# Attention's row maxima: four columns turned by one product into four padding rows, placed by a masked multiply on VectorE

## What is computed

```python
def causal_block_attention(q, k, v, log_decay_cum=None):
    T = q.shape[1]
    scale = q.shape[-1] ** -0.5
    ...
    for blk in range(T // Q_BLOCK):
        lo, hi = blk * Q_BLOCK, (blk + 1) * Q_BLOCK
        s = jnp.einsum('bqhd,bkhd->bhqk', q[:, lo:hi], k[:, :hi]) * scale
        if log_decay_cum is not None:
            s = s + (cum[:, :, lo:hi, None] - cum[:, :, None, :hi])
        mask = (lo + jnp.arange(Q_BLOCK))[:, None] >= jnp.arange(hi)[None, :]
        p = jax.nn.softmax(jnp.where(mask, s, -jnp.inf), axis=-1)
        outs.append(jnp.einsum('bhqk,bkhd->bqhd', p, v[:, :hi]))
    return jnp.concatenate(outs, axis=1)
```

## Time and profile before

| | us |
|---|---|
| median of three runs | 2696.1 |
| lowest and highest | 2695.87, 2705.18 |
| span of the profiled execution | 2699.1 |
| TensorE busy | 2458.8 |
| VectorE busy | 1280.1 |
| ScalarE busy | 972.9 |
| GpSimd busy | 862.0 |

### The profile page before, as it was taken

One profiled execution on the slowest core, in us unless ns is written; L12 is line 12 of the kernel. 1 busy time (PEld: TensorE's weight loads), 2 busy tenths in 40 slices (PEclk: granted clock), 3 DMA queues, 4 the chain that ended last, 5 costly groups with the idle time before them and its releaser, 6 DMA issues.

```text
span 2699.1 us, 32797 instructions
## 1 busy us (share of the span) xinstructions
PE 2458.8 (91%) x13104; PEld 1870.4 (69%) x13104; DVE 1280.1 (47%) x1966; ACT 972.9 (36%) x1596; POOL 862.0 (32%) x726
## 2 busy tenths in 40 slices
PE   7977699998999999899999766999989999998998
PEld 7755477897577695655697555779865866856556
DVE  4049934543514325565431698236344153265653
ACT  4232214632433433344433222155324243333441
POOL 1225522211441620154411455121205225202542
PEclk9988899999999999999999888999999999999999
DMA  4100043041010021200321000422300101122003
GB/s 137 51 0 1 1 132 107 17 156 47 1 48 1 13 74 57 95 23 1 126 79 35 1 1 1 160 79 69 135 16 1 48 1 45 42 89 85 1 1 117
DMA packets 91864, 141.15 MB, mean 52 GB/s; under 512 B 18208, under 2 KB 65344, under 8 KB 91712
## 3 DMA queue, kind: packets, MB, share of 16 engines
q1 hardware_dynamic: 91712, 139.05, 15.1%
HBM read 105.48 MB, written 33.55 MB: 52 GB/s over the span
## 4 chain that ended last, share of the span: by engine, by line
PE 79%; DVE 15%; issue 3%; ACT 2%; POOL 1%; DMA 0%; POOLq 0%; SPq 0%; DVEq 0%; ACTq 0%
PE psum L227 36%; PE psum L478 12%; PE psum L1379 6%; PE psum L1364 4%; PE psum L1333 3%; PE psum L1365 3%; PE psum L1367 3%; PE psum L864 3%; PE psum L1346 2%; PE psum L1318 2%; DVE gla_E L703 2%; DVE gla_ql L666 2%; DVE gla_A L724 2%; PE psum L1386 1%; DVE gla_S L756 1%
## 5 line engine op out<-in xcount | busy, mean ns | idle before, releaser
L193 POOL TENSOR_TENSOR w_lo<-w_raw,w_hi 128x2048 fp32r<-128x2048 f32 (+3 forms) x60 | 278.2, 4638 | 970.5 <-ACT w_hi L186 970.5
L864 PE MATMUL psum<-gla_ql,gla_kl 128*128 128x256 f32 x448 | 147.5, 484 | 115.4 <-DVE gla_ql L666 111.7
L864 PEld LDWEIGHTS psum<-gla_ql,gla_kl 128*128 128x128 f32 x448 | 105.8, 248 | 162.1 <-DVE gla_A L724 112.4
L227 PE MATMUL psum<-h_hi,w_hi 128*128 128x512 f32 x768 | 199.3, 403 | 0.0
L1577 POOL TENSOR_TENSOR mla_acc<-mla_acc,mla_p 128x512 f32<-128x512 f32 (+3 forms) x160 | 160.2, 1015 | 107.9 <-ACT mla_p L1447 106.5
L227 PE MATMUL psum<-w_hi,h_hi 128*128 128x256 f32 (+3 forms) x1280 | 186.2, 289 | 4.7 <-ACT w_hi L186 4.7
L227 PE MATMUL psum<-h_lo,w_hi 128*128 128x512 f32 x768 | 190.1, 390 | 0.0
L227 PE MATMUL psum<-h_hi,w_lo 128*128 128x512 f32 x768 | 189.8, 390 | 0.0
L227 PE MATMUL psum<-w_hi,h_lo 128*128 128x256 f32 (+3 forms) x1280 | 182.2, 286 | 0.0
L227 PE MATMUL psum<-w_lo,h_hi 128*128 128x256 f32 (+3 forms) x1280 | 179.8, 283 | 1.8 <-POOL w_lo L193 1.8
L186 ACT ACTIVATE w_hi<-w_raw 128x2048 fp32r<-128x2048 f32 (+3 forms) x60 | 113.4, 1894 | 187.1 <-PE psum L478 174.3
(11 more groups left out here) (321 smaller groups left out, 4827.7 us busy)
## 6 DMA issues: line engine op xcount, KB each, us to landing
w_raw<-in_w_in_dram SPq DMA_DIRECT2D x38, 1024.0 KB, 5.2
out_dram<-x_rows SPq DMA_DIRECT2D x64, 512.0 KB, 2.7
x_rows<-out_dram SPq DMA_DIRECT2D x56, 512.0 KB, 5.6
w_raw<-in_w_out_dram SPq DMA_DIRECT2D x16, 1024.0 KB, 5.2
x_first<-in_x_dram SPq DMA_DIRECT2D x8, 512.0 KB, 7.4
x_rows<-in_x_dram SPq DMA_DIRECT2D x8, 512.0 KB, 6.6
w_raw<-in_w_in_dram SPq DMA_DIRECT2D x2, 1088.0 KB, 8.9
w_raw<-in_w_in_dram SPq DMA_DIRECT2D x2, 1056.0 KB, 5.1
```

Source lines behind the costliest of these rows:

```text
L193: pool.tensor_tensor(self.w_lo[c["set"]][:, :n], self.w_raw[c["set"]][:, :n], self.w_hi[c["set"]][:, :n].bitcast(F32), ALU.subtract).then_ ...
L227: last = pe.matmul(o, lhs, rhs, start=(kk == 0 and n == 0), stop=(kk == KT - 1 and n == 2))
L864: last = pe.matmul(k.psum[:, n % self.NB, g * HH * self.HALF:(g + 1) * HH * self.HALF], self.kl[:, m % self.R, g, :], self.ql[:, m % self. ...
```

## The change

TensorE turns the four columns with one product: the four columns are its weights, and the result is four rows (partitions 96 to 99) of 128. VectorE then multiplies, for each of the four blocks of 128 columns, all four rows by a column of the 4 by 4 identity, and writes four rows of 512: row 96 + x holds the maxima of block x in block x and zeros elsewhere. Rows 96 to 99 of `k_hi` hold ones, and the first product of `scores_turned` goes over 100 rows instead of 97. `place_max` leaves ScalarE's queue and enters VectorE's, behind the maxima of the same unit and ahead of `refine`, `out` and the hook; in `begin_dve` it stands behind the last maximum.

```diff
-M_ROW = 96
+M_ROW, M_END = 96, 100
...
-        for x in range(4):
-            last = pe.matmul(k.psum[M_ROW:M_ROW + 1, self.misc_bank("m", i, a), x * P:(x + 1) * P],
-                             self.nmax[:, i, a, x:x + 1], k.ident[:, :], start=True, stop=True)
-        last.then_inc(self.m_turned.sem, 1)
+        pe.matmul(k.psum[M_ROW:M_END, self.misc_bank("m", i, a), :P], self.nmax[:, i, a, :], k.ident[:, :], start=True,
+                  stop=True).then_inc(self.m_turned.sem, 1)
...
-        k, R = self.k, M_ROW + 1
+        k, R = self.k, M_END
...
-    def place_max(self, act, i, a):
-        p, c = self.items[i]
-        act.wait_ge(self.m_turned.sem, self.m_turned.at(2 * i + a + 1))
-        act.activation(self.q_hi[(2 * p + c) % self.QS][M_ROW:M_ROW + 1, a, :],
-                       self.k.psum[M_ROW:M_ROW + 1, self.misc_bank("m", i, a), :], ACT.Copy).then_inc(self.m_done.sem, 1)
...
-                if self.m_at(i, j) is not None:
-                    self.place_max(act, i + 1, self.m_at(i, j))
...
-                last = dve.memset(self.k_hi[i][M_ROW:M_ROW + 1, :, :].bitcast(F32), 1.0)
+                last = dve.memset(self.k_hi[i][M_ROW:M_END, :, :].bitcast(F32), 1.0)
...
+    def place_max(self, dve, i, a):
+        p, c = self.items[i]
+        r = slice(M_ROW, M_END)
+        dve.wait_ge(self.m_turned.sem, self.m_turned.at(2 * i + a + 1))
+        dve.tensor_tensor(self.q_hi[(2 * p + c) % self.QS][r, a, :].rearrange("r (x q) -> r x q", x=4),
+                          self.k.psum[r, self.misc_bank("m", i, a), :P].unsqueeze(1).to_broadcast([4, 4, P]),
+                          self.k.ident[r, r].unsqueeze(2).to_broadcast([4, 4, P]), ALU.mult).then_inc(self.m_done.sem, 1)
...
                 for n in self.scores_at(i, j):
                     self.maximum(dve, i + 1, n)
+                if self.m_at(i, j) is not None:
+                    self.place_max(dve, i + 1, self.m_at(i, j))
                 if i and j == 4:
                     self.refine(dve, i - 1)
```

More of the change, by code:

```diff
@@ L1460, in begin_act @@
             self.round_group(act, 0, g)
-        for a in range(2):
-            self.place_max(act, 0, a)
     def scalar(self, act, hook=None):
@@ L1544, in begin_dve @@
                 self.rest_of_group(dve, 0, groups[n // 2])
+        for a in range(2):
+            self.place_max(dve, 0, a)
     def vector(self, dve, hook=None):
```

## The result

The changed kernel is slower: 2761.0 us median of four runs (2756.1 to 2763.9) against 2697.3 of the kernel before on the same chip; the ratio is 1.0228, with a 95% interval of 1.0212 to 1.0245. The forecast was 2687.0, with a range to 2701. The span of the profiled execution went from 2699.1 to 2762.0 us.

A forecast was written before the change was run, and what follows sets the result against it. TensorE bounds the kernel where its queue is dense, VectorE where TensorE waits for it. Per layer 7.75 us gained, 15.5 for two, less 6.4 for the clock: 9.1 off the median 2696.1, so 2687.0 us, range 2674 to 2701.

The forecast's parts named there:

- Six records at 0.108 us: TensorE, each of 64 places: six of eight turn records go, 6 x 0.108 = 0.65 us a place.
- free borders: Item ends where VectorE has only the placements to do: six borders of two places per layer, 7.8 us gained.
- placement was costed at 0.68 us: VectorE, 64 new multiplies: 0.68 us each, between 0.59 and 0.746.
- that rival (0.06): VectorE's placement held up by GpSimd, 0.6 us more each: 2704, or 2715 with lower clock; chance 0.06.
- tight border: End of c = 0 items, i > 0: join, `out`, two placements in a row; 0.2 us left of 1.3.
- waits behind the hooks: `attC`, TensorE: nearly 3 us at unit 1 of item 1, some 3.6 in item 2; losses 1.4 and 1.3.
- wait for the rotation: `attC`, item 2 to 3: wait of 2.71 us, put off by 0.67 by one placement; loss 0.9 us.
- the beginnings: Attention starts, unit 0 earlier: 2.0 us gained in `att1` and `att0`, 0.35 in `attC`, together 2.35 per layer.
- half speed: Beginning of `att0`: unit 0 starts 1.65 us earlier but takes 1.6 instead of 0.81; about 1.0 us gained.
- the price of a low stretch: TensorE's clock at 0.60 for 4 us after a long wait: 1.6 us each, 3.2 per layer, 6.4 in all.
- more low stretches: Clock also falls at 8 tight borders and 6 beginnings, 1.6 us each: 2695 to 2709.4; chance 0.17.
- 1.3 + 1.6 more: Item 2 of `attC`: 1.3 us lost to two placements ahead of a maximum, 1.6 to the lowered clock.

The follow-up runs named there:

- dense beginnings: Changed kernel plus three more products, results not read, in each turn of an attention's first item: 2714.3 us, ratio 1.0050.
- three pairs: Without and with dense first-item turns: changed kernel 2761.0, 2714.3; one product, placement on ScalarE 2742.1, 2693.4; kernel before with the change in first items only 2744.4, unchanged 2697.6.
- ScalarE kernel: Changed kernel with the placement as four copies on ScalarE, and three more unread products in each first-item turn: 2693.4 us, ratio 0.9977.
- 8 records: Changed kernel plus one more unread product in each first-item turn, 8 records in place of 16: 2714.8 us, ratio 1.0069.

## Why the prediction was wrong

**What held.** Six records at 0.108 us: at the free borders the next unit starts 0.31 us after the start of the turn instead of 0.96, and with dense beginnings an item with two such places came down from 26.2 to 24.9 us, 1.3, to the tenth. The placement was costed at 0.68 us and took 0.697, the same in all 64, of which 36 run beside a GpSimd instruction; that rival (0.06) is out. The Trainium skill's rule ("SBUF — State Buffer", Who interferes with whom), that a VectorE instruction with at most one SBUF input does not contend with GpSimd, agrees: 0.698 us at the longest. A tight border kept nothing (19.6 + 19.6 became 18.9 + 20.3; 0.2 was forecast), and a placement releases unit 1 there, as the order of time of the changed kernel shows:

```profile
748.66 0.70 DVE L1513 TENSOR_TENSOR fox_q_hi<-psum,ident 4x512 fp32r<-4x512 f32 x1
...
749.39 0.69 DVE L1535 TENSOR_TENSOR fox_gate<-psum,fox_gate 128x512 f32<-128x512 f32 x1
...
750.11 0.70 DVE L1513 TENSOR_TENSOR fox_q_hi<-psum,ident 4x512 fp32r<-4x512 f32 x1
...
750.87 0.50 PE L1362 MATMUL psum<-fox_q_hi,fox_k_hi 100*128 100x512 f32 x1 [0.47 <-DVE fox_q_hi L1513]
```

The waits behind the hooks, forecast at nearly 3 and at 3.6 us, are 3.10 and 3.60. They were read in the kernel with dense beginnings. In the changed kernel itself the first shows in the second layer alone (3.11 us), where the clock was back before the end of item 0; in the first layer item 0 still runs at the lower clock when it meets that hook. The wait for the rotation grew from 2.71 to 4.09 us.

**Step that failed first: the beginnings.** The sum had them at 2.35 us gained per layer, and took "half speed" only for what unit 0 gave up. The place was right (1.8 us saved up to unit 0 of `att1`), the clock behind it wasn't asked for. The earlier trace rows showed the low clock during the 16 records, and the earlier trace rows full clock elsewhere; the row that was missing is the stretch just behind the 16 records, which is at 1.00. I read the low stretch as something that passes by itself. The runs show that with these records it ends and without them it goes on: six beginnings cost 47 to 49 us in each of three pairs, where 4.7 us of gain stood in the sum. (That gain was also added up a little high: 1.65 us less the 0.8 that unit 0 gives up is 0.85, not 1.0, 0.3 us a layer.)

**Step that failed second: the price of a low stretch, 1.6 us.** It came from one row of a stretch that dense work followed. Behind the waits of 3.10 and 4.09 us, also ahead of dense work, the ten microseconds of 1146 to 1156 and 1204 to 1214 of the kernel with dense beginnings are at 0.66 and 0.79; by the prediction's own working, 10 x 0.34 and 10 x 0.21, that is 3.4 and 2.1 us. The rival "more low stretches" had the right mechanism and put the beginnings among its places, but with that price it ended at 2709. Ahead of sparse work the stretch lasts much longer, ten microseconds or more in item 2 of `attC` and some 30 at the beginning of `att1`: in FoX first items went from 18.8 (dense beginning) to 26.5 us, 7.7 us instead of 1.6, and item 2 of `attC` from 19.8 to 25.6 or 26.3 instead of 1.3 + 1.6 more. With the 36 products added back, the attentions sum to 713.1 us, 7.9 over the kernel before: `attC` pays 9.3 twice, the four FoX attentions gain 10.7.

**What else the sum left out.** In `attC` the gain of the free places was thought to be kept. TensorE gets to the hooks earlier and waits there longer, even when VectorE has nothing added (0.77 to 2.08 us in the ScalarE kernel), and the longer wait lowers the clock where the shorter one did not. The tight borders lowered it at one of eight: item 3 of the first `att1` took 23.4 us, with the clock at 0.50 from 752 to 756.

**Settled, and open.** That the clock of the beginnings is the cause of 47 us is shown, by adding the products to the changed kernel and by taking them from the kernel before. No run puts a bare delay of the same length in their place. That it is the products and not the later start of unit 0 that brings the clock back is therefore argued: in the kernel with dense beginnings the clock returns within some half a microsecond of the end of the 16 records each time, and behind TensorE's idle times of 2 to 4 us in `attC` it fell. That VectorE's share of the change costs some 20 us is shown by the ScalarE kernel (2714.3 against 2693.4, both with dense beginnings); by the item durations it is 17.0, of which 15.7 lie in `attC`. With both causes taken away the kernel is 7 us faster than the kernel before, which had 2700.3 beside it. The theory's other half, that a sparse item doesn't bring the clock back by itself, is too strong. In the second `attC` of the changed kernel it was back at 2527, in the item that began at 2511, and with 8 records it came back inside the fifth first item; what decides it is open. Why the clock comes back behind 8 records at some beginnings and not at others is open, as is the reason why run times of two kernels can differ by less than their attentions do (3 against 14.7 us).

## What to carry to other kernels

Before taking products off TensorE, look at the granted clock during them and right behind them, and at how dense the work is that follows: products that look superfluous can be what gives the clock back to a sparse stage, and 36 of them were worth 47 us here. Price a low stretch by the length of the sparse work behind it, not by the one row in which it was seen to end. A stage that gets faster on one engine reaches the blocks in the next engine's queue earlier; unless these are broken up, the gain turns into a wait there, and moving the block alone moves only the wait.

## What was unexpected of the hardware

A sparse stage can be held at 1.2 GHz although TensorE looks busier in it than at full clock: 18.52 of 20 us busy at 0.52, against 18.07 at 0.92, in the rows of the first items above. It stayed so for up to some 40 us, from 1138 to 1178 in the first `attC` of the changed kernel, the last 8 us of it in the dense item 1. The Trainium skill ("TensorE: Matmul & The Clock Gate", What's actually happening) says that "the default state is throttled, and activity releases the throttle", and these rows agree. The same section puts the penalty of the ramp, which it tells of a kernel's first products, at under 1% of a typical span; here, where the clock fell again at six stages in the middle of the kernel, they made 1.7%.

Fewer products took longer, repeatably: 12720 records in 2761.0 us, 12792 in 2714.3. And in one execution the same 8 records were followed by full clock at some beginnings and by 0.50 for a whole item at others.
